# A hybrid attention, convolution and mixture-of-experts block: modulation group 9 moved ahead of the input statistics, groups 8 to 15 summed in fours

## The reference, cut to what matters

```python
mods_x = jnp.split(silu(c) @ w_mod + b_mod, 6)      # shift, scale, gate for attention; the same for the FFN
nx = rmsnorm(h_x, attn_norm) * (1 + sca_x) + sa_x   # the context tokens likewise
q_a, kv_a, k_rope, g_b, g_c, hh = split(nx @ w_in)  # 512, 256, 64, 1024, 1024, 1024 columns
o_conv = g_b * conv3(g_c * hh)                      # depthwise over tokens, width 3
o_mla  = attention(rmsnorm(q_a) @ w_q_b, rmsnorm(kv_a) @ w_kv_b, rotary)
h = h_x + ga_x * (concat(rmsnorm(o_mla), rmsnorm(o_conv)) @ w_out)
h = h + gf_x * moe(modulated_norm(h, ffn_norm, sf_x, scf_x))
out = rmsnorm(h, final_norm)
```

## Time and profile before

| | us |
|---|---|
| runs of the kernel before | 1110.08 median (1109.07 to 1110.6) |
| the profiled execution | 1106.52 |
| its span | 1104.6 |
| TensorE matmul busy | 1010.1 (91%) |
| VectorE busy | 551.4 (50%) |
| ScalarE busy | 223.2 (20%) |
| GpSimd busy | 23.9 (2%) |
| moved by DMA | 380.34 MB, mean 344 GB/s |

### The profile page before, as it was taken

The page is one execution under the profiler, slowest core; times in us unless marked ns, Lnnn a source line. Parts: engine busy times, 40 slices in busy tenths (PEclk is TensorE's granted clock), DMA queues, the critical chain, the costliest instruction groups (busy, mean ns, idle before and its releaser), DMA issues.

```text
span 1104.6 us, 15716 instructions
## 1 busy us (share of the span) xinstructions
PE 1010.1 (91%) x6042; PEld 565.5 (51%) x6043; DVE 551.4 (50%) x1094; ACT 223.2 (20%) x451; POOL 23.9 (2%) x33
## 2 busy tenths in 40 slices
PE   3999998999999889999999999988899898998975
PEld 2644487888885345444485645433343333433421
DVE  3100359754824694985582335544346334544523
ACT  5311120000002363010241212221112203213212
POOL 1000010000002001000000000000000000000002
PEclk9999998999999999999999999999899998999998
DMA  9999998999855747999739999999999999999994
GB/s 356 391 390 388 350 358 264 371 354 327 284 182 172 255 144 261 387 387 334 235 108 383 399 409 408 409 408 407 409 409 407 408 407 409 409 407 409 409 405 166
DMA packets 158362, 380.34 MB, mean 344 GB/s; under 512 B 10498, under 2 KB 44112, under 8 KB 157136
## 3 DMA queue, kind: packets, MB, share of 16 engines
q1 hardware_dynamic: 158288, 379.35, 91.6%
HBM read 377.22 MB, written 2.10 MB: 343 GB/s over the span
## 4 chain that ended last, share of the span: by engine, by line
PE 65%; DMA 13%; SPq 9%; DVE 9%; issue 3%; ACT 1%; POOL 0%; DVEq 0%; POOLq 0%; ACTq 0%
PE ps L674 64%; DMA ring<-in_w_exp_down 8%; SPq L547 4%; DVE part L1664 4%; SPq L542 3%; DMA ring<-in_w_mod 3%; DMA qkv<-in_w_mod 1%; DVE tiny L1851 1%; DVE xres L2136 1%; SPq L553 1%; DMA ring<-in_w_exp_up 1%; DVE kq L1614 0%; PE ps L748 0%; ACT nreg L1477 0%; DVE nreg L1614 0%
## 5 line engine op out<-in xcount | busy, mean ns | idle before, releaser
L674 PE MATMUL ps<-nreg,ring 128*128 128x256 f32 (+2 forms) x1312 | 307.7, 398 | 4.2 <-DVE ring L1856 4.1
L674 PEld LDWEIGHTS ps<-nreg,ring 128*128 128x128 f32 (+1 forms) x1312 | 243.7, 190 | 63.5 <-issue 30.6
L1664 DVE SCALAR_TENSOR_TENSOR part<-ring,csT,part 128x512 f32<-128x512 f32 x232 | 174.7, 753 | 9.2 <-DMA ring<-in_w_mod 0.3
L674 PE MATMUL ps<-ring,nreg 128*32 128x512 f32 (+1 forms) x1344 | 173.4, 599 | 3.4 <-DMA ring<-in_w_exp_up 3.0
L674 PE MATMUL ps<-ring,conv 128*32 128x512 f32 (+2 forms) x688 | 103.5, 656 | 23.7 <-DMA ring<-in_w_exp_down 22.9
L674 PE MATMUL ps<-ring 128*128 128x512 f32 x256 | 110.7, 592 | 0.0
L674 PEld LDWEIGHTS ps<-ring,nreg 128*32 128x32 f32 (+1 forms) x1344 | 48.6, 114 | 111.0 <-issue 110.9
L2136 DVE TENSOR_TENSOR xres<-xres,ps 128x512 f32<-128x512 f32 x96 | 61.6, 683 | 48.5 <-PE ps L674 48.5
L674 PEld LDWEIGHTS ps<-ring 128*128 128x128 f32 x256 | 48.6, 190 | 60.4 <-issue 60.0
L674 PEld LDWEIGHTS ps<-ring,conv 128*32 128x32 f32 (+2 forms) x688 | 29.5, 125 | 89.2 <-issue 85.5
L674 PE MATMUL ps<-nreg,conv 128*128 128x512 bf16 x228 | 57.9, 379 | 11.8 <-DVE xres L2136 8.7
(11 more groups left out here) (285 smaller groups left out, 864.5 us busy)
## 6 DMA issues: line engine op xcount, KB each, us to landing
ring<-in_w_mod SPq DMA_DIRECT2D x78, 1024.0 KB, 11.1
ring<-in_w_exp_gate SPq DMA_DIRECT2D x128, 512.0 KB, 13.6
ring<-in_w_exp_up SPq DMA_DIRECT2D x128, 512.0 KB, 15.2
ring<-in_w_exp_down SPq DMA_DIRECT2D x128, 512.0 KB, 14.5
ring<-in_w_in SPq DMA_DIRECT2D x12, 2048.0 KB, 13.0
ring<-in_w_out SPq DMA_DIRECT2D x8, 2048.0 KB, 11.7
ring<-in_w_mod SPq DMA_DIRECT2D x3, 2048.0 KB, 18.0
ring<-in_w_in SPq DMA_DIRECT2D x3, 1664.0 KB, 16.2
```

Source lines behind the costliest of these rows:

```text
L674: return nc.tensor.matmul(o, l, r, start=start, stop=stop)
L1664: ins = V.scalar_tensor_tensor(out=out_, in0=w_, scalar=scale, in1=acc_, op0=ALU.mult, op1=ALU.add)
```

## The change

Two things. Group 9 is accumulated in front of the statistics; its loads stand ahead of the load of block B of step 0. And groups 8 to 15 are summed four at a time: when four groups are accumulated, `quad_sums` multiplies each by a 128 x 32 piece of ones into its own 32 rows of bank 5 (512 columns, so every one of the 32 rows holds the sums), ScalarE copies the bank to `quad_rows` (in `kq`), `quad_cols` transposes it in four pieces and VectorE's `quad_features` picks one column for each group. The first four are finished in step 2, the second four behind the second projection. `sorted_part` has four buffers. The steps 1 to 3 are written out on TensorE, VectorE and ScalarE; SyncE keeps its loop.

```diff
--- before.py
+++ after.py
@@ -179,7 +179,8 @@
         tblT = brow[:, :]
         places = crow[:, 0:2 * NE]
         counted = part[:, 0, :]
-        sorted_part = qnT[:, 0:4, :].rearrange("p h t -> p (h t)").rearrange("p (b n) -> p b n", b=2)
+        sorted_part = qnT[:, :, :].rearrange("p h t -> p (h t)").rearrange("p (b n) -> p b n", b=4)
+        quad_rows = kq[:, 1536:2048]
         blocks, sums = part[:, 1, 0:128], part[:, 1, 128:192]
 
         WI = KR0 + ROPE
@@ -456,8 +457,8 @@
             load_group(8, 12, mslot, freed_by_pe)
             sp.wait_ge(shift_full, 2)
             load_conv(0, 1, CONV0 + 2 * CW)
+            load_group(9, 13, mslot, freed_by_dve)
             load_conv(0, 2, CONV0)
-            load_group(9, 13, mslot, freed_by_dve)
             with sp.Fori(1, 4) as i:
                 sp.wait_ge(conv_full, 6 * i - 4)
                 load_conv(i, 0, CONV0 + CW)
@@ -694,12 +695,20 @@
                 pe.wait_ge(acc_done, 16 * (n - 8) + 16)
                 pe.wait_ge(modT_done, n)
 
-            def mod_sum_cols(n, b):
-
-                mod_sum(n)
+            def quad_sums(a):
+
+                pe.wait_ge(acc_done, 64 * a + 64)
+                pe.wait_ge(modT_done, 4 * a + 8)
+                for v in range(4):
+                    ins = mm(ps[32 * v:32 * v + 32, 5, :], ones[:, 0:32], sorted_part[:, v, :], True, True)
+                ins.then_inc(mod_rows, 1)
+
+            def quad_cols(a):
+
+                pe.wait_ge(part_full, 9 + a)
                 for j in range(4):
-                    ins = mm(ps[:, 5, j:j + 1], sorted_part[:, b, 128 * j:128 * j + 128], ones[:, 0:1], True, True)
-                ins.then_inc(mod_cols, 1)
+                    ins = nc.tensor.transpose(ps[:, 5, 128 * j:128 * j + 128], quad_rows[:, 128 * j:128 * j + 128], ident)
+                ins.then_inc(mod_cols, 4)
 
             def mod_sum_wide(n):
 
@@ -870,22 +879,21 @@
             conv_blocks(0, 1, BANKS_H, (0,))
             in_squares()
             conv_blocks(0, 1, BANKS_H, (1,))
-            pe.wait_ge(kv_out, 2)
-            mod_sum_cols(8, 0)
             pe.wait_ge(gc_out, 2)
             pe.wait_ge(mean_wide, 2)
             conv_blocks(0, 2, BANKS_B)
-            mod_sum_cols(9, 1)
-            with pe.Fori(1, 4) as i:
+            pe.wait_ge(kv_out, 2)
+            for i in range(1, 4):
                 conv_blocks(i, 0, BANKS_C, (0,))
-                pe.wait_ge(modT_done, 2 * i + 8)
+                if i == 2:
+                    quad_cols(0)
+                pe.wait_ge(y_out, 2 * i)
                 conv_blocks(i, 0, BANKS_C, (1,))
                 conv_blocks(i, 1, BANKS_H)
-                mod_sum_cols(2 * i + 8, 0)
                 pe.wait_ge(gc_out, 2 * i + 2)
-                pe.wait_ge(mean_wide, 2)
                 conv_blocks(i, 2, BANKS_B)
-                mod_sum_cols(2 * i + 9, 1)
+                if i % 2:
+                    quad_sums(i // 2)
             pe.wait_ge(y_out, 8)
             pe.wait_ge(kr_done, 1)
 
@@ -913,6 +921,8 @@
                     lhs = [[w[:, k, h + u, NOPE:NOPE + ROPE] for u in range(2)] if rope else [w[:, k, h, 0:NOPE]]
                            for k in range(4)]
                     project(6 * s + n, T, [(lhs[k], qaT[:, k, :]) for k in range(4)])
+                    if s == 0 and n == 1:
+                        quad_cols(1)
                     if n == 3:
                         rotate(2 * s)
                 rotate(2 * s + 1)
@@ -1375,13 +1385,22 @@
             square_root(rowkv)
 
 
-            with sc.Fori(0, 4) as i:
-                sc.wait_ge(modT_done, 2 * i + 8)
+            def quad_out(a):
+
+                sc.wait_ge(mod_rows, 9 + a)
+                copy(quad_rows, ps[:, 5, :]).then_inc(part_full, 1)
+
+            for i in range(4):
+                if i:
+                    sc.wait_ge(u_out, 2 * i)
+                if i == 2:
+                    quad_out(0)
                 for m in range(2):
                     sc.wait_ge(conv_full, 6 * i + m + 1)
                     copy(gcs[:, m, :], ps[:, BANKS_C[m], 0:T]).then_inc(gc_out, 1)
 
 
+            quad_out(1)
             for j in range(0, 28, 2):
                 sc.wait_ge(proj_full, j + 1)
                 bank = ps[:, j % 4, :]
@@ -1648,7 +1667,7 @@
                 acc = part[:, b, :]
                 for q in quarters:
                     if q == ks[0] == 0:
-                        ve.wait_ge(mod_cols, n - 1)
+                        ve.wait_ge(mod_cols, n - 1 if n < 10 or n >= ATT_GROUP + 2 else 8 if n < 14 else 12 if n < 16 else 16)
                     if ks[0] == 0:
                         ve.wait_ge(m_full[q], 16 * (n - 7))
                     for k in ks:
@@ -1659,16 +1678,17 @@
                             ve.wait_ge(acc_done, 16 * (n - 8) + (4 * q + k))
                             out_, w_, acc_ = acc, w, acc
                             if by_feature and q == k == 3:
-                                out_, w_, acc_ = (by_row(sorted_part[:, b, :], 128).rearrange("p j c -> p c j"),
+                                out_, w_, acc_ = (by_row(sorted_part[:, n % 4, :], 128).rearrange("p j c -> p c j"),
                                                   w.rearrange("p (c j) -> p c j", j=4), acc.rearrange("p (c j) -> p c j", j=4))
                             ins = V.scalar_tensor_tensor(out=out_, in0=w_, scalar=scale, in1=acc_, op0=ALU.mult,
                                                          op1=ALU.add)
                         ins.then_inc(acc_done, 1)
 
-            def sum_out(n, g):
-
-                ve.wait_ge(mod_cols, n + 1)
-                V.tensor_copy(modT[:, bass.ds(4 * g, 4), 0:1], ps[:, 5, 0:4].unsqueeze(2)).then_inc(modT_done, 1)
+            def quad_features(a):
+
+                ve.wait_ge(mod_cols, 4 * a + 12)
+                V.tensor_copy(modT[:, 48 + 16 * a:64 + 16 * a, 0:1].rearrange("p (v c) a -> p v (c a)", v=4),
+                              ps[:, 5, :].rearrange("p (c v r) -> p v c r", c=4, v=4)[:, :, :, 0]).then_inc(modT_done, 4)
 
             def gate_out(n, bank=5):
 
@@ -1747,6 +1767,7 @@
 
             kv_gain(0)
             kv_gain(1)
+            accumulate(9, 1, by_feature=True)
             ve.wait_ge(stat_full, 1)
             ve.wait_ge(kr_mm, 1)
             ve.wait_ge(q_out, 4)
@@ -1793,23 +1814,23 @@
 
             def conv_products(i):
 
-                sum_out(2 * i + 8, 2 * i + 12)
                 for m in range(2):
                     ve.wait_ge(conv_full, 6 * i + 5 + m)
                     V.tensor_tensor(oT[:, bass.ds(8 + m + 2 * i, 1), :].rearrange("p a t -> p (a t)"), ps[:, BANKS_B[m], 0:T],
                                     ycv[:, m, :], ALU.mult).then_inc(y_out, 1)
-                sum_out(2 * i + 9, 2 * i + 13)
-
-            accumulate(9, 1, by_feature=True)
-            conv_rows(0)
-            conv_products(0)
-            with ve.Fori(1, 4) as i:
-                accumulate(2 * i + 8, 0, by_feature=True)
-                accumulate(2 * i + 9, 1, by_feature=True)
+
+            for i in range(4):
+                for n in range(2 * i + 8, 2 * i + 10) if i else ():
+                    if n == 12:
+                        ve.wait_ge(mod_rows, 9)
+                    accumulate(n, n % 2, by_feature=True)
+                    if n == 12:
+                        quad_features(0)
                 conv_rows(i)
                 conv_products(i)
             steps[0] += 4 * LINKS
 
+            quad_features(1)
             ve.wait_ge(modT_done, 16)
             ve.wait_ge(cols_in, 48)
             link(V.tensor_tensor(modT[:, 48:80, 0:1], modT[:, 48:80, 0:1], bT2[:, :].unsqueeze(2), ALU.add))
```

## The result

The changed kernel takes 1103.55 us, median of 5 runs (1101.11 to 1105.27), against 1110.08 (1108.02 to 1111.47): ratio 0.9940, interval 0.9923 to 0.9957. In the comparison that it shares with the first experiments it is 1102.85 against 1109.22, ratio 0.9935 (0.9921 to 0.9950). So 6.4 to 6.5 us were gained by the medians where 8.4 were forecast. The profiled execution took 1105.27 us, its span 1103.4.

A forecast was written before the change was run, and what follows sets the result against it. TensorE alone was taken to bound the 185 us from the convolution's start. Gains of 2.0 (stall), 2.6 (clock) and 3.8 (sums) make 8.4 us, carried to the end: median 1101.7 us against 1110.08, range 1098.8 to 1106.5.

The forecast's parts named there:

- Group 9 in the idle stretch: VectorE accumulates group 9 before the statistics; TensorE's 4.90 us stall becomes 2.9 us before block B, gaining 2.0 us.
- The clock: TensorE's clock stays up after the 2.9 us idle time before block B, gaining 2.6 us; little over even odds.
- rival 1: The clock drops in the new idle time before block B, costing 1.7 us: 1103.4 us; chance 0.33.
- Sums: Eight column sums, 6.48 us, become two row sums and two sets of transposes, 2.70 us (2.6 to 3.4): gain 3.78.
- The written-out loop: Steps 1 to 3 written out, 41.63 us a step on TensorE without the sums: neither gain nor loss.
- the covers: Other work hides the added waits, costed at nothing; without VectorE's cover for groups 12 and 13, 0.6 us twice.
- The lead at the first projection: TensorE's first projection comes at about 309.3 us, against 318.18 before.
- second transposes: The last set of transposes, behind the second projection, takes 0.5 us back from the gain.
- the old stall: TensorE idles 4.90 us behind block B of step 0; with the low clock (0.89 + 1.71) it costs 7.50 us.
- a lead that isn't there at the end: Sign against the forecast: the lead at the first projection missing at the end; 8.4 us was carried there.
- the stall's part of the sum: Moving group 9 turns 4.90 us of idling into 2.9, gaining 2.0 us, plus 2.6 if the clock stays up.
- the exchange of the wait: Step 0's wait for group 9's column becomes one for the products, met under the C block: costed at nothing.

The follow-up runs named there:

- the first experiments: The four runs after_again, move_only, sums_only and copies_first, from one comparison with the kernel before, 1109.22 us there.
- late_work: The changed kernel with eight more filling products on TensorE in front of the router's transposes: 1106.49 us, 0.9972 to the kernel before.
- unrolled_only: The kernel before with steps 1 to 3 written out on TensorE, VectorE and ScalarE and nothing else: 1109.28 us against 1108.82, 1.0005.
- after_again: The changed kernel unaltered, run and traced once more: 1102.85 us, 0.9935 to the kernel before.
- move_only: The kernel before with only group 9 and its loads moved, old column sums and loops kept: 1104.14 us against 1109.22, 0.9962.
- sums_only: The changed kernel with the move of group 9 undone, row sums and written-out loop kept: 1098.98 us, 0.9902 to the kernel before.
- copies_first: The changed kernel with ScalarE's two C copies of step 0 ahead of the kv root: 1100.97 us, 0.9918 to the kernel before.
- late_sum: The kernel before, each step's second column sum behind the next C block, the wait there for products instead of columns: 1101.87 us against 1109.16, 0.9935.
- kv_mean_first: The changed kernel with ScalarE's C copies ahead of the kv root and VectorE's kv mean behind the query mean: 1098.20 us against 1109.16, 0.9900.
- sums_loads: sums_only with the H block's load of step 1 ahead of group 10's on SyncE's queue: 1098.27 us against 1109.16, 0.9912.

## Why the prediction was right, and where its reasons were not

**Group 9 in the idle stretch: right.** Start 148.4 forecast, 148.15 measured (less the 2.1 us); statistics 3.5 us late forecast, 3.1 measured; idle time 2.9 forecast, 2.42, 2.74 and 2.48 in the three traces, released by ScalarE's copies each time.

**The clock: the likelier case was the other one.** The forecast took it to stay up after 2.9 us, with little over even odds; rival 1 was that it drops, for 1.7 us. In the three traces of the changed kernel it dropped each time, for 1.7 us, in late_work it didn't. Rival 1's time, 1103.4, is what was measured (1103.55 and 1102.85), but that it fits so well is luck: the lead at the first projection was larger than rival 1 has it, and more was lost behind it. Both follow.

**Sums: right.** Row sums took 1.00 and not 0.86 us, transposes 0.43 and 0.5: 3.0 us in all and not 2.7, within the bounds. The 1.00 against 0.86 leaves 0.14 us for going in and out together. The Trainium skill, TensorEngine Tiling (Array Packing), Key Properties, says that a change of tiling mode drains the engine; the trace agrees as far as there is something to pay, and it is no more than that.

**The written-out loop at nothing: right**, by unrolled_only, and so were the covers: TensorE has no idle time from block B to the attention.

**The lead at the first projection: 8.2 us, forecast 8.9 at full clock and 7.2 with a drop.** The forecast had the first projection at 309.3 against 318.18; its 8.4 are what it expected behind the second transposes. The 1.0 us by which the measured lead beats the case with a drop lies in two terms. One is the idle time, 2.4 to 2.7 us and not 2.9. The other is the old stall, whose 7.5 us were taken from one trace. The idle time is steady there, the drop behind it is not: the 128 records that took 29.58 us took 30.77 and 30.43 in the other two traces of before, so the stall cost 8.7 and 8.3 us in them.

```profile
186.97 30.77 PE L674 MATMUL ps<-nreg,ring 128*128 128x256 f32 x128
```

**From there to the end: 1.7 to 1.8 us of the 8.2 are lost, which the forecast had at 0.5.** The prediction named a lead that isn't there at the end as a sign against it; what is missing is small beside its range, and the range holds the measured time. Three things can be seen in the traces. The expert stretch is none of them: at 534 to 538 us it can't be told apart in the two kernels.

1. The second transposes, as forecast: from first projection to first expert load the changed code takes 252.4 to 252.6 us where no clock drops, the code of before 252.0 to 252.1.
2. A late start ahead of the change. Group 7's transposes begin at 126.05 to 126.60 us in the six traces with column sums and at 126.88 to 127.03 in six of the eight with row sums, whether group 9 is moved or not; the other two, the first and the third trace of the changed kernel, have the drop of the clock at 99.6 us on top. By the means of the six and the six it is 0.6 us, against every kernel with row sums. In all eight TensorE waits 0.4 to 0.8 us at 97 us for a load for which it doesn't wait in the six. The code up to there is the same, and unrolled_only doesn't have the delay, so it isn't the written-out loop; why the load lands later isn't known.
3. A second drop of the clock, in the attention, behind an idle time that is the same in every trace. TensorE and slices in after_again:

```profile
387.08 3.41 PE L675 MATMUL ps<-nreg,ring 128*128 128x256 f32 x8 [2.17 <-DVE ring L1877]
```

```profile
386.00:388.00 2.00, 0.92 (x3) 0.83 (x4) 1.93 (x5) 1.35 (x4) 0.00 (x0) 0.86 0.83 321
388.00:390.00 2.00, 2.00 (x6) 1.56 (x6) 1.97 (x5) 0.10 (x2) 0.00 (x0) 0.50 0.28 39
```

In the first trace of after the same eight records behind the same wait took 1.97 us at clock 1.00, as in the earlier trace rows. A drop there costs 1.4 to 1.6 us (254.0 and 254.2 against 252.6 from first projection to first expert load). The second and third trace of the changed kernel have it, and late_work, move_only, sums_only and copies_first. The traces of late_sum, kv_mean_first and sums_loads do not, though they come there as early, and neither do the four traces that come there late, the three of before and unrolled_only. Whether an earlier start makes it more frequent (6 of 10 against none of 4) or it is chance, these traces don't tell; this is left open.

8.2 less 0.4 and 0.6 is 7.2 us without the drop in the attention and 5.7 with it, and the 6.4 to 6.5 of the medians lie between. How often the clock drops in the executions without a trace isn't on record.

**What the prediction had wrong is which edit brings the gain.** It made the move carry the stall's part of the sum: "4.90 us of idling become 2.9", and the clock's 2.6 us on top. It priced the column sums at their own 0.81 us each, and the exchange of the wait ("Step 0's wait for the column of group 9 becomes one for the products, met under the C block") it put among the waits that are costed at nothing. But the stall stood in front of a column sum. With that sum out of the place between blocks B and C, and the wait exchanged, TensorE is free: late_sum has these two alone and gains 7.3 us, 8.3 at the first projection, which is the old stall (7.5, 8.7 and 8.3 us in the three traces). The runs don't part the place of the sum from the exchange of the wait. The move gains 5.1 us where the sum stands (move_only) and loses 3.9 where it doesn't (sums_only against the changed kernel), since then it only puts ScalarE's copies behind 3 us of VectorE. The two edits overlap. The sum for both came out right since the prediction followed the changed kernel's own order of events. Split by edits it comes near for the move (2.0 + 2.6 forecast, 5.1 measured) and is far off for the sums: 3.8 forecast, 10.2 measured.

**The better kernel.** The row sums without the move (0.9902) or with it and the kv mean and copies ahead (0.9900) beat both kernels, by 10.2 and 11.0 us against before and by about 4 against the changed one.

## What to carry to other kernels

When a change takes away a wait and also moves what the wait was for, price each edit with the other left out: here a reduction whose result nobody needed soon stood in TensorE's order ahead of 7 us of independent work, and putting it behind that work gave all that the move gave. Work pushed into an engine's idle stretch delays what stands behind it; follow that to the last small copy that frees a bank, on another engine. And an idle time of TensorE of some 1.6 to 2.3 us is priced with and without a drop of the clock, since here both happened. Last, a drop's cost read from one trace is one sample: behind the same stall it was 1.7, 2.9 and 2.6 us on the same work.

## What was not expected of the hardware

Behind short idle times of TensorE the granted clock fell to half or stayed up, in the same place of the same program. Of the first 560 us of the 14 traces:

| idle time | clock stayed full | fell to half |
|---|---|---|
| 1.5 to 1.8 us | 21 | 4 |
| 1.9 to 2.3 us | 10 | 10 |
| 2.4 to 2.8 us | 0 | 3 |
| 4.9 us | 0 | 4 |

The shortest that was followed by a drop was 1.55 us (move_only), the longest that was not 2.30 us (late_work). The price of a drop was 1.4 us for the eight records in the attention (3.41 against 1.97) and 1.7 us for block B and what follows. The Trainium skill, TensorE: Matmul & The Clock Gate, in its table of why this matters, puts the limit for idle gaps higher than the shortest of these; the measurement decides.
